# Convolution taps of GpSimd and ScalarE moved to VectorE, and the rounding of the softplus sums to ScalarE

## The reference, cut to what matters

```python
proj = h @ w_in                                   # glu, q k v, gates
u = u_val * sigmoid(u_gate)                       # 512 channels
u = causal_depthwise_conv(u, conv_w, conv_b)      # 31 taps per channel
u = silu(layernorm(u, conv_ln_g, conv_ln_b))
y_conv = u @ w_conv_out
# stick-breaking attention, 8 heads
z = q k^T / 8
log_keep = where(causal, log_sigmoid(-z), 0)      # = -softplus(z)
log_after = reverse_cumsum(log_keep) - log_keep
a = where(causal, exp(log_sigmoid(z) + log_after), 0)
o = a @ v
merged = sigmoid(g_conv) * y_conv + sigmoid(g_att) * (o @ w_att_out)
```

## Time and profile before

| what | us |
|---|---|
| median of three runs | 1374.23 |
| lowest and highest | 1372.99, 1374.35 |
| the profiled execution | 1373.22 |
| its span | 1371.4 |
| TensorE busy in it | 1344.5 |
| VectorE | 986.8 |
| ScalarE | 714.9 |
| GpSimd | 180.9 |

### The profile page before, as it was taken

The page is one execution under the profiler, slowest core; times in us unless marked ns, Lnnn a source line. Parts: engine busy times, 40 slices in busy tenths (PEclk is TensorE's granted clock), DMA queues, the critical chain, the costliest instruction groups (busy, mean ns, idle before and its releaser), DMA issues.

```text
span 1371.4 us, 19821 instructions
## 1 busy us (share of the span) xinstructions
PE 1344.5 (98%) x7788; PEld 1170.3 (85%) x7788; DVE 986.8 (72%) x1390; ACT 714.9 (52%) x1170; POOL 180.9 (13%) x167
## 2 busy tenths in 40 slices
PE   9999999999999999999999999999999999999997
PEld 7888888788769999998887778887778999998885
DVE  6799899678587878878326764677787788776322
ACT  4466886553475555573224543557465555564221
POOL 3388343200010000004000011121000000000000
PEclk9999999999999999999999999999999999999998
DMA  9422112455701332324532144543221323333221
GB/s 368 146 92 93 47 47 77 148 183 184 299 16 62 100 117 93 122 94 155 176 100 89 62 127 121 133 112 89 95 74 34 121 93 117 100 108 108 92 92 62
DMA packets 45310, 155.98 MB, mean 114 GB/s; under 512 B 6049, under 2 KB 6305, under 8 KB 45090
## 3 DMA queue, kind: packets, MB, share of 16 engines
q1 hardware_dynamic: 42882, 149.70, 32.9%
q0 software_dynamic: 2336, 5.01, 1.6%
HBM read 143.39 MB, written 2.10 MB: 106 GB/s over the span
## 4 chain that ended last, share of the span: by engine, by line
PE 88%; DVE 7%; ACT 3%; issue 1%; POOL 0%; DVEq 0%; ACTq 0%; POOLq 0%
PE ps L1741 27%; PE ps L1742 26%; PE ps L1743 26%; PE ps L1891 1%; DVE t_buf L1098 1%; PE ps L1829 1%; DVE w_lo L1064 1%; PE ps L2157 1%; PE ps L1783 1%; PE ps L1794 1%; PE ps L1795 1%; PE ps L1799 1%; DVE h_lo L1090 1%; ACT w_hi L578 1%; PE ps L2125 0%
## 5 line engine op out<-in xcount | busy, mean ns | idle before, releaser
L1741 PE MATMUL ps<-h_hi,w_hi 128*128 128x256 f32 (+1 forms) x1120 | 374.0, 334 | 3.0 <-ACT sq L806 1.1
L1743 PE MATMUL ps<-h_hi,w_lo 128*128 128x256 f32 (+1 forms) x1120 | 371.6, 332 | 0.0
L1742 PE MATMUL ps<-h_lo,w_hi 128*128 128x256 f32 (+1 forms) x1120 | 371.4, 332 | 0.0
L1064 DVE TENSOR_TENSOR w_lo<-raw,w_hi 128x1024 fp32r<-128x1024 f32 x141 | 183.7, 1306 | 115.6 <-ACT w_hi L578 114.4
L1741 PEld LDWEIGHTS ps<-h_hi,w_hi 128*128 128x128 f32 x1120 | 212.8, 190 | 27.1 <-issue 3.5
L1743 PEld LDWEIGHTS ps<-h_hi,w_lo 128*128 128x128 f32 x1120 | 212.8, 190 | 20.3
L1742 PEld LDWEIGHTS ps<-h_lo,w_hi 128*128 128x128 f32 x1120 | 212.9, 190 | 19.4 <-issue 0.5
L578 ACT ACTIVATE w_hi<-raw 128x1024 fp32r<-128x1024 f32 x141 | 148.1, 1055 | 147.1 <-PE ps L1743 74.0
L1054 DVE TENSOR_TENSOR w_lo<-quads,w_hi 128x1024 fp32r<-128x1024 f32 (+1 forms) x152 | 164.8, 1085 | 72.7 <-ACT w_hi L578 72.7
L578 ACT ACTIVATE w_hi<-quads 128x1024 fp32r<-128x1024 f32 (+1 forms) x152 | 144.3, 949 | 78.2 <-PE ps L1743 76.6
L1741 PE MATMUL ps<-act_hi,w_hi 128*128 128x512 f32 x352 | 137.0, 389 | 0.0
(11 more groups left out here) (316 smaller groups left out, 2262.3 us busy)
## 6 DMA issues: line engine op xcount, KB each, us to landing
quads<-in_ffn_in SPq DMA_DIRECT2D x76, 512.0 KB, 4.5
raw<-in_ffn_out SPq DMA_DIRECT2D x44, 512.0 KB, 3.7
raw<-in_ada SPq DMA_DIRECT2D x32, 512.0 KB, 4.2
raw<-in_qk SPq DMA_DIRECT2D x25, 512.0 KB, 3.7
ada<-in_ada SPq DMA_DIRECT2D x16, 512.0 KB, 7.6
raw<-in_gates SPq DMA_DIRECT2D x16, 512.0 KB, 3.7
raw<-in_v SPq DMA_DIRECT2D x12, 512.0 KB, 3.7
raw<-in_ffn_in SPq DMA_DIRECT2D x12, 512.0 KB, 3.9
```

The lines of the kernel that those rows point to most:

```text
L1064: nc.vector.tensor_tensor(w_lo[SLOT[p]][:], raw[q % RAW][:], w_hi[SLOT[p]][:].bitcast(f32), ALU.subtract).then_inc(raw_used, 1)
L1741: nc.tensor.matmul(out, w[0], v[0], start=start, stop=False, **kw)
L1742: nc.tensor.matmul(out, w[0], v[1], start=False, stop=False, **kw)
L1743: return nc.tensor.matmul(out, w[1], v[0], start=False, stop=stop, **kw)
```

## The change

All 124 taps go to VectorE, in an order that goes round all four channels: four behind each q and k tile, two for each v panel, three, eight for each head, five behind the feed of gate 9 and the last twelve behind that of gate 10. GpSimd's adds, ScalarE's products and the buffers between them are gone. The rounding to `sb_hi` moves to ScalarE as `sum_hi_part(h)`, behind `weight(h-1)`. VectorE's softplus is cut in two: `softplus(h)` makes the sums, and `softplus_lo(h)` takes the low half and frees `sp_ready`; it stands behind the feed and behind `a_lo` of the head before. The diff, without the declarations of buffers and semaphores:

```diff
-        TAP_ORDER = [(c, j) for j in range(TAPS) for c in range(2)]
+        TAP_ORDER = [(c, j) for j in range(TAPS) for c in range(CT)]
-        SUM_ORDER = [(c, j) for j in range(1, TAPS) for c in range(2, CT)]
 # GpSimd
-            for n, (c, j) in enumerate(SUM_ORDER):
-                pool.wait_ge(tap_prod, n + 3)
-                if n >= 2:
-                    pool.wait_ge(pool_tap, n - 1)
-                nc.gpsimd.tensor_tensor(conv[:, c, :], conv[:, c, :], tap_buf[n % 3][:], ALU.add).then_inc(pool_tap, 1)
 # ScalarE
-            def first_taps(): ...
-            def products(n): ...
             for i in range(8):
                 prepare("qk1", i)
-                if i == 0:
-                    first_taps()
                 qk_tile("qk1", i, QK1_BANK[i], QK[i], i % 2, qk_hi)
-                products(3)
+            def sum_hi_part(h):
+                act.wait_ge(sp_part, 3 * (h + 1))
+                if h:
+                    act.wait_ge(c_done, h)
+                nc.scalar.activation(sb_hi[:], sb_e[:], ACT.Copy).then_inc(sb_hi_ready, 1)
             for b in range(1, 4):
                 prepare("v1", b)
-                products(3)
+                if b == 1:
+                    sum_hi_part(0)
             for h in range(HEADS):
                 weight(h)
+                if h + 1 < HEADS:
+                    sum_hi_part(h + 1)
                 if h:
                     head_out(h - 1, qk_hi, pv_done, o_hi)
                 prepare("gates", h + 1)
                 if h + 1 < HEADS:
                     gate_tile(h + 1)
-                    products(3)
             head_out(HEADS - 1, qk_hi, pv_done, o_hi)
-            products(4)
             gate_tile(KT)
             for i in range(KT + 1, 2 * KT):
                 prepare("gates", i)
-                if i == 9:
-                    products(len(SUM_ORDER))
                 gate_tile(i)
 # VectorE
             for i in range(8):
                 feed("qk1", i)
                 qk_lo_tile("qk1", i, QK1_BANK[i], QK[i], i % 2, qk_hi, qk_lo, i + 1)
-                taps(2)
+                taps(4)
             def softplus(h):
...
+            def softplus_lo(h):
+                dve.wait_ge(sb_hi_ready, h + 1)
                 if h:
                     dve.wait_ge(c_done, h)
-                dve.wait_ge(sp_part, 3 * (h + 1))
-                link(nc.vector.tensor_copy(sb_hi[:], sb_e[:]))
                 nc.vector.tensor_tensor(sb_lo[:], sb_e[:], sb_hi[:].bitcast(f32), ALU.subtract).then_inc(sp_ready, 1)
             for b in range(4):
                 feed("v1", b)
-                taps(1)
+                taps(2)
+                if b == 0:
+                    softplus(0)
                 if b == 1:
-                    softplus(0)
+                    softplus_lo(0)
...
                 nc.vector.tensor_tensor(a_lo[:], sb_a[:], a_hi[:].bitcast(f32), ALU.subtract).then_inc(a_ready, 1)
+                if h + 1 < HEADS:
+                    softplus_lo(h + 1)
                 if h:
                     head_lo(h - 1, qk_hi, qk_lo, o_hi, o_ready)
-                taps(4)
+                taps(8)
...
                 feed("gates", i)
-                if i == 9:
-                    taps(len(TAP_ORDER))
+                if i <= 10:
+                    taps(5 if i == 9 else len(TAP_ORDER))
 # TensorE
                     pe.wait_ge(tap, len(TAP_ORDER))
-                    pe.wait_ge(pool_tap, len(SUM_ORDER))
```

More of the change, by code:

```diff
@@ L185, in build @@
         tri_f = place("tri_f", [P, P], f32, at=A0 + 93 * K)
-        tap_buf = [place(f"tap_buf{i}", [P, SEQ], f32, at=A0 + 94 * K + 2 * K * i) for i in range(3)]
         gate_a = place("gate_a", [P, KT, SEQ], f32, at=A0 + 48 * K)
@@ L254, in build @@
         glu_done, glu_sig, u_ready = sem("glu_done"), sem("glu_sig"), sem("u_ready")
-        mod_one, mod_ready, pool_tap = sem("mod_one"), sem("mod_ready"), sem("pool_tap")
-        tap_prod = sem("tap_prod")
+        mod_one, mod_ready, sb_hi_ready = sem("mod_one"), sem("mod_ready"), sem("sb_hi_ready")
         hi_of = {n: sem(f"hi_of_{n}") for n in ("qk1", "v1", "qk2", "v2", "v3", "qk3")}
@@ L1240, in _ @@
             dve.wait_ge(u_ready, CT)
+            dve.wait_ge(consts, 10)
             for i in range(8):
```

## The result

The kernel after takes 1397.32 us in the median of four runs (1396.22 to 1398.14), the kernel before in the same comparison 1373.64 us. The ratio is 1.0172, with a 95% interval from 1.0154 to 1.0189: 23.7 us slower. The prediction said 1391.4 us, a range up to 1397, and slower with 0.90. The sign and the mechanism came as forecast; the time is 5.9 us above the forecast and 0.3 us above the range.

The account below looks back on a forecast made before the run. TensorE, busy 98% of the span, was taken as the bound. Delays 2.3 + 1.2 + 7.1 + 4.2 - 1.0 + 3.4 = 17.2 us on 1373.22, plus 1.0 for the median, gave 1391.4 us, range 1384 to 1397.

Parts of the forecast that it names:

- part 1: Operations that go and come: 124 VectorE taps at 0.67 us, 83 us against 70.2, VectorE's load about unchanged.
- part 2: q and k projections, 71 to 111 us: VectorE's 4.5 us per tile under TensorE's 5.4, cost 0.
- part 3: Head loop: TensorE's release comes last after VectorE-ScalarE hand-overs, 14.4 us a head against 12.63, +14.8 us in all.
- part 4: Last suffix sums to the convolution's mean: last product with V +13.8 us late, mean waiting for taps, +17.2.
- rival D: TensorE's clock falls behind waits: 3.0 us at the mean, 1394.4 us; two or three falls 1397 to 1400; chance 0.15.
- the likeliest case: Head loop and late last taps delay TensorE by 17.2 us, clock unchanged: 1391.4 us, chance 0.61.
- Rival C: Head loop: w_hi ready within 8.6 us of the release, TensorE keeps its pace, not slower: 1372.6 us, chance 0.10.
- Rival B: Head loop: taps are covered and ScalarE sets a 13.2 us cycle, +10.6, 1384.8 us; chance 0.12.

Follow-up runs that it names:

- e1: Kernel after with VectorE's feed of the next gate panel moved behind a_lo and softplus_lo, same loads: 1380.25 us, ratio 1.0044.
- e5: Kernel after with four taps a head in place of eight, 32 taps left out of the convolution: 1392.23 us, ratio 1.0134.
- e8: Kernel after with ScalarE rounding the weight panel (w_hi) ahead of the softplus sums, VectorE's order unchanged: 1380.87 us, ratio 1.0059.
- e2: Kernel after with 71 small unused matmuls on TensorE ahead of its waits: 1391.1 us, ratio 1.0126.
- e3: Kernel before with all 124 taps on VectorE, rounding left as a cast in VectorE's old place: 1379.02 us, ratio 1.0040.
- e4: Kernel before with only the rounding moved to ScalarE and softplus_lo in the new order, taps divided as before: 1395.7 us, ratio 1.0157.
- e10: e4 with small unused matmuls on TensorE ahead of its waits for sb_lo: 1392.44 us, ratio 1.0133.
- e9: Kernel after with VectorE's softplus_lo and head_lo ahead of the feed and more taps placed early: 1371.15 us, ratio 0.9979.

## Why the prediction missed by 6 us

**Load (part 1): right.** Eight taps take 5.38 us, 0.67 each as priced. The mean of the 120 taps that are no first ones is 743 ns (81.3 us), and GpSimd does nothing in the stretch.

```profile
L1149 DVE SCALAR_TENSOR_TENSOR conv<-u_pad,cols,conv 128x512 f32<-128x512 f32 x120 | 81.3, 743 | 0.1
```

**Projections (part 2): right.** No wait appears there. The first suffix sums start at 139.92 us, 0.5 earlier than before, but that is scatter: in e1, e5 and e8, which run the same program up to there, they start at 141.90 to 141.95. So the heads are counted from there.

**Head loop (part 3): right in mechanism and nearly in size.** From the first suffix sums on, each head costs against before +2.15 (forecast 2.3), +1.0 (1.2), then 14.50, 14.59, 14.50 and 15.67 us where I had 14.4, and 14.49 for the last (+4.25, forecast 4.2). The one that stands out, 15.67, has the clock at half in it. With the clock held up (e2) it is 14.60. The hand-overs are not why my cycle is 0.1 to 0.2 us short: in the head shown they take 0.04 and 0.03 us, as priced. ScalarE's rounding and head out take 1.29 and 0.62 us from start to start (173.81, 175.10, 175.72), where I had 1.18 and 0.47; smaller terms take some of that back. I had forecast some 15 us of waits for sb_lo and 11.3 came: behind two falls TensorE is itself late, and its wait shrinks to 0.34 and 0.25 us. A sum of waits understates the loss there.

**Last suffix sums to the mean (part 4): right.** In e2, 11.2 us from the last suffix sums to the last product (241.13 to 252.35), forecast 11.0; the wait at the mean is 3.39 us, forecast 3.4. In after the first of these takes 14.16 us (240.15 to 254.31).

**The step that failed is the clock, rival D, for which the sum of the likeliest case had no term.** I gave it 0.15, priced it only behind the longest wait, at the mean (3.0 us), and put two or three falls at the far edge, outside of the range. It fell four times in the stretch. What each cost, by rows of after against e2: the head from 209.99 to 225.66, 15.67 - 14.60 = 1.1 us; the last suffix sums to the last product, 14.16 - 11.22 = 2.9; the mean, 4.83 against 3.13 (274.24 to 277.37), 1.7. The fall at 181.7 us cost nothing: the next suffix sums still come 14.59 us later, and only the wait ahead of them shrinks, from 1.80 to 0.34 us. Sum 5.7 us, which is also the difference of the stretch times (141.1 and 135.4 us); the medians of after and e2 are 6.2 apart. The missing term is that size, and my sum without it, 1391.4, is near what e2 ran at. That these agree within 0.3 us is partly luck: by the stretch time e2 is 18.0 us slower than before, 0.8 more than my 17.2.

The reason I gave against D, that no row showed a fall behind a wait, was true of the rows and worth little. The kernel before has hardly any waits, so it could hardly show one; one that has seven is another regime. And its trace holds a hint that my rows left out: about 3 us ahead of the fall of the earlier trace rows TensorE waits, for 0.83 us before 794.38, and short matmuls follow.

The Trainium skill ("TensorE: Matmul & The Clock Gate", "Why this matters for your kernels") had warned of gaps between bursts. The runs agree: the clock fell at waits in after and stayed up where e2 filled them. Two of the four falls stand at waits of 1.80 us (ahead of 180.90 and of 209.99), in heads that each have a wait; the other two at 4.10 and 3.39.

Rival C was wrong as forecast: w_hi was done 10.4 us after the release, as reckoned, and VectorE did stand waiting for it. Its condition, w_hi within 8.6 us, is met in e8 (8.3 us), and there the heads 2 to 6 do run at TensorE's 12.63; in e1 one moved line makes the condition needless. Rival B is the cycle of e5, where four taps are missing, not of after.

**What stays open.** Which pattern of idle time makes the clock fall. Two waits of 1.80 us came with a fall, and the single one of 2.19 us in e3, while one of 2.08 us, at 150.7, the 2.0 us in e1 and the 2.3 us at the start of before did not. The same wait of 2.08 us in e5, which does the same as after up to there, did come with one (it begins at about 155.3 us), so the same work can come with a fall or without. And what e4 would take with the clock up: e10 was built too full to say.

## What to carry to other kernels

When a step moves to another engine, write out each engine's queue in order and ask where in it the instruction stands that releases the bottleneck: behind a request that the other engine answers late, it pays that request's whole delay in every round, while the busy shares fall. Move the release to the front before counting loads; here one moved line was worth 18 us, the falls of the clock that went with its waits included, while 62 more taps cost 4.7 us in e3 and nothing in e9, where they are spread. And when a change gives the bottleneck engine its first regular waits, price its clock in those waits and in the work behind them, as part of the likeliest case; fillers that end before the wait does tell the two apart.

## What was not expected of the hardware

- TensorE's clock fell four times in 140 us, twice at a wait of only 1.80 us, and stayed low for up to 7 us, and in e4 it fell in every second head. It cost 5.7 us of 23.7 by the rows, 6.2 by the medians.
- A fall costs only where TensorE, or an engine that waits for its results, sets the pace: 0 us in one head, 2.9 behind the last suffix sums. In the head that took 15.67 us ScalarE waited for the slowed suffix sums:

```profile
215.41 1.36 ACT L669 ACTIVATE sb_a<-ps 128x512 f32<-128x512 f32 x3 [1.41 <-PE ps L1872]
```

- 71 matmuls that nobody needs made the kernel after 6.2 us faster.
